# The low-rank pass in blocks of 480 columns, and the first unit's loads, splits and products in one program part with the first norm

## The reference, cut to what matters

```
xn = rmsnorm(x, norm_mix_pre)
p  = xn @ w_in          # RWKV r,k,v (3 x 2048), low-rank w,a,g (96+96+256), DeltaNet q,k,v, z, beta, alpha (16+16), two gates
y_A = RWKV-7 time mixing; decay, a and gate come from the low-rank columns: tanh(lw) @ w2, la @ a2, sigmoid(lg) @ g2
y_B = gated DeltaNet; beta = sigmoid(p_beta), g = -exp(a_log) * softplus(p_alpha + dt_bias)
x  = x + rmsnorm((sigmoid(gA) * y_A + sigmoid(gB) * y_B) @ w_out)
x  = x + rmsnorm(swiglu(rmsnorm(x)))
```

## Time and profile before

| | |
|---|---|
| median of 3 runs | 2353.65 us |
| the profiled execution, its own time | 2358.39 us |
| its span, first to last instruction | 2356.5 us |
| mean granted TensorE clock | 0.948 |
| TensorE matmuls busy | 2161.3 us (92%) |
| VectorE, ScalarE, GpSimd busy | 1414.1, 1086.9, 158.2 us |

### The profile page before, as it was taken

How to read it: one execution, slowest core, us unless ns; L and a number is a source line. 1 busy time by engine, 2 the same in 40 slices (tenths; PEclk the granted TensorE clock), 3 DMA queues, 4 the chain that set the end, 5 groups by cost and what they waited for, 6 DMA issues and landing times. The chain is left out here.

```text
span 2356.5 us, 51465 instructions
## 1 busy us (share of the span) xinstructions
PE 2161.3 (92%) x19523; PEld 1862.1 (79%) x19523; DVE 1414.1 (60%) x2772; ACT 1086.9 (46%) x2019; POOL 158.2 (7%) x277
## 2 busy tenths in 40 slices
PE   5699999999999999999999966939999999999995
PEld 5698888888888888888888854838888888878884
DVE  3276687778677766867776754444554544444444
ACT  4354555545554545555454533344444444434443
POOL 2000110110011011101101110000000000000000
PEclk8699999999999999999999966969999999999998
DMA  4654545444444545444544304426655555545452
GB/s 114 155 143 116 138 111 132 123 125 125 115 116 123 129 113 139 113 113 123 130 114 113 87 5 185 154 90 197 195 182 192 181 192 182 174 165 191 178 184 101
DMA packets 388239, 327.32 MB, mean 139 GB/s; under 512 B 15360, under 2 KB 328160, under 8 KB 381408
## 3 DMA queue, kind: packets, MB, share of 16 engines
q1 hardware_dynamic: 376304, 319.16, 46.5%
q10 hardware_dynamic: 11760, 5.41, 0.9%
HBM read 322.44 MB, written 2.10 MB: 138 GB/s over the span
## 5 line engine op out<-in xcount | busy, mean ns | idle before, releaser
L1489 DVE TENSOR_TENSOR wlo<-wr,whi 128x1024 fp32r<-128x1024 f32 x296 | 362.4, 1225 | 436.0 <-ACT whi L1484 436.0
L232 PE MATMUL ps<-hi,xh 128*128 128x384 f32 (+1 forms) x1600 | 581.7, 364 | 42.8 <-DVE lo L218 24.4
L234 PE MATMUL ps<-hi,xl 128*128 128x384 f32 (+1 forms) x1600 | 548.9, 343 | 0.0
L233 PE MATMUL ps<-lo,xh 128*128 128x384 f32 (+1 forms) x1600 | 548.1, 343 | 0.0
L1484 ACT ACTIVATE whi<-wr 128x1024 fp32r<-128x1024 f32 x296 | 313.5, 1060 | 493.2 <-PE ps L1502 484.9
L218 DVE TENSOR_TENSOR lo<-raw,hi 128x768 fp32r<-128x768 f32 (+1 forms) x400 | 378.1, 964 | 147.6 <-ACT hi L213 144.0
L213 ACT ACTIVATE hi<-raw 128x768 fp32r<-128x768 f32 (+1 forms) x400 | 328.1, 834 | 245.8 <-PE ps L234 235.4
L232 PEld LDWEIGHTS ps<-hi,xh 128*128 128x128 f32 x1600 | 311.1, 194 | 76.4 <-issue 47.7
L1498 PE MATMUL ps<-whi,xh 128*128 128x512 f32 x832 | 328.1, 394 | 20.5 <-DVE wlo L1489 20.5
L1502 PE MATMUL ps<-whi,xl 128*128 128x512 f32 x832 | 326.9, 393 | 0.0
L1500 PE MATMUL ps<-wlo,xh 128*128 128x512 f32 x832 | 326.5, 392 | 0.0
(11 more groups left out here) (284 smaller groups left out, 2396.1 us busy)
## 6 DMA issues: line engine op xcount, KB each, us to landing
raw<-in_w_in SPq DMA_DIRECT2D x294, 512.0 KB, 5.5
wr<-in_ffn_w_gate SPq DMA_DIRECT2D x44, 1024.0 KB, 5.2
wr<-in_ffn_w_up SPq DMA_DIRECT2D x44, 1024.0 KB, 5.2
wr<-in_ffn_w_down SPq DMA_DIRECT2D x22, 2048.0 KB, 7.7
wr<-in_w_out SPq DMA_DIRECT2D x16, 1024.0 KB, 5.2
xt<-in_x SPq DMA_DIRECT2D x1, 2048.0 KB, 8.0
x<-in_x SPq DMA_DIRECT2D x1, 2048.0 KB, 15.8
out_x<-y SPq DMA_DIRECT2D x1, 2048.0 KB, 7.0
```

The lines of the kernel that those rows point to most:

```text
L232: nc.tensor.matmul(o, xh[:, kc, xs], hi[q % QBUF][:, k, 0:w], start=kc == 0, stop=False)
L233: nc.tensor.matmul(o, xh[:, kc, xs], lo[q % QBUF][:, k, 0:w], start=False, stop=False)
L234: last = nc.tensor.matmul(o, xl[:, kc, xs], hi[q % QBUF][:, k, 0:w], start=False, stop=kc == KC - 1)
L1489: nc.vector.tensor_tensor(wlo[s.par][:], src, whi[s.par][:].bitcast(F32), ALU.subtract).then_inc(s.lo, 1)
```

## The change

1. The low-rank pass is cut by contraction blocks: 16 quanta of one block with all 480 columns (`project_lora`, 6 matmuls of 480 columns each), in 4 fills of 4 blocks, each loaded by three transfers (224, 224 and 32 columns).
2. SyncE's list of part 1 begins with x in two halves, each with its own semaphore, then the four low-rank fills, then the six fills of unit 0. The 14 row loads, the 7 small loads and unit 0's 5 small weights are issued by ScalarE, at three places of its list. TensorE's wait for the parameter rows counts these 14 alone (`rows_in`); the rows are turned in PSUM bank 7.
3. The norm: a root chain for each half of x, and x is scaled on VectorE. VectorE first copies the parameters (`par`).
4. TensorE waits before a low-rank quantum for the xl group that it reads, not for the last. The first four hi splits and the first lo split stand ahead of the transposes.
5. Unit 0's 20 splits, 18 quanta and two take-outs move from part 2 to part 1, around the tail; the barrier stands behind them.

```diff
-                    sp.dma_start(xt[:], a["x"][0].rearrange("(t p) n -> p t n", p=P)).then_inc(x_in, 16)
...
+                    for t in range(NT):
+                        sp.dma_start(xt[:, t, :], a["x"][0][t * P:(t + 1) * P, :]).then_inc(x_in[t], 16)
                     for fill in range(4):
...
+                        for at, col, n in ((0, COL_LORA, 224), (224, COL_LORA + 224, 224), (448, COL_BETA, 32)):
...
+                    load_unit_weights(sp, 0)
...
+        def project_lora(pe, q):
+
+            pe.wait_ge(lo_ready, count(None, q + 1))
+            for t in range(NT):
+                last = product(ps[:, 4 + t, 0:LW], q, t, split_of(hi, None, q), split_of(lo, None, q))
             last.then_inc(quantum_done, 1)
...
+                    dve.wait_ge(Pe.sem, Pe.after("par"))
+                    step("par", nc.vector.tensor_copy(par2[:, 0:352], ps[:, 7, 0:352]))
+                    for t in range(NT):
+                        one = slice(t, t + 1)
+                        dve.wait_ge(A.sem, A.after(f"ss{t}"))
+                        step(f"var{t}", nc.vector.tensor_scalar(ss[:, one], ss[:, one], 1.0 / D, NORM_EPS, ALU.mult, ALU.add))
+                        rsqrt(nc, dve, D_, f"rs{t}_", 0, rx[:, one], ss[:, one], rt[:, one])
+                        D_.step(f"xs{t}", nc.vector.tensor_scalar(xt[:, t, :], xt[:, t, :], rx[:, one], None, ALU.mult))
+                    split_lo(dve, None, 0)
                     transpose_x_dve(dve, D_, A, NORM1)
...
-                    pe.wait_ge(D_.sem, D_.after("lo7"))
                     for q in range(QL):
-                        project(pe, None, q, PW if q < 8 else 96)
+                        pe.wait_ge(D_.sem, D_.after(f"lo{q // 2}"))
+                        project_lora(pe, q)
+                    for q in range(4):
+                        project(pe, 0, q)
                     pe.wait_ge(pass_out, 2)
...
+                    for q in range(4, FIRST):
+                        project(pe, 0, q)
```

More of the change, by code:

```diff
@@ L136, in build @@
         small_in = sem("small_in")
+        rows_in = sem("rows_in")
         tiles = sem("tiles")
-        x_in = sem("x_in")
+        x_in = [sem(f"x_in{i}") for i in range(2)]
         masks_made = sem("masks_made")
@@ L268, in transpose_x_pe, with transpose_x_act @@
                 done.step(f"x{g}", last)
-        def transpose_x_act(act, done, turned, weight):
-            for g in G8:
+        def transpose_x_act(act, done, turned, weight, groups=G8):
+            for g in groups:
                 act.wait_ge(turned.sem, turned.after(f"x{g}"))
@@ L354, in _ @@
[L354 to L360, removed]
@@ L449, in _ @@
                                                               accum_out=ss[:, t:t + 1]))
-                    act.wait_ge(D_.sem, D_.after("rs10"))
-                    for t in range(NT):
-                        A.step(f"xs{t}", nc.scalar.activation(xt[:, t, :], xt[:, t, :], ACT.Copy,
-                                                              scale=rx[:, t:t + 1]))
-                    act.wait_ge(D_.sem, D_.after("par"))
-                    transpose_x_act(act, A, Pe, NORM1)
-                    for q in range(QL):
-                        split_hi(act, None, q, PW if q < 8 else 96)
@@ new lines, in _ @@
+                    split_hi(act, None, QBUF)
+                    with nc.allow_non_contiguous_dma(reason="a few hundred single values"):
+                        for i, (c0, n) in enumerate(lora_cols):
+                            act.dma_start(lmix[0:n, i:i + 1],
+                                          mix[3 * D + c0:3 * D + c0 + n].rearrange("(p a) -> p a", a=1)
+                                          ).then_inc(small_in, 16)
+                    act.dma_start(alog[:], a["gdn_a_log"][0].partition_broadcast(P)).then_inc(small_in, 16)
@@ L464, in _ @@
+                    act.wait_ge(quantum_done, QL)
+                    for t in range(NT):
+                        nc.scalar.activation(lp[:, t, :], ps[:, 4 + t, 0:LW], ACT.Copy).then_inc(pass_out, 1)
+                    for q in range(2, 6):
+                        split_hi(act, 0, q)
                     act.wait_ge(Pe.sem, Pe.after("lora"))
@@ L527, in _ @@
                         ALU.mult, ALU.mult))
+                    for q in range(11, FIRST + LEAD):
+                        split_lo(dve, 0, q)
                 @block.tensor
@@ L1428, in _ @@
                 def _(act):
-                    for q in range(FIRST + LEAD):
-                        split_hi(act, 0, q)
-                        if q % 8 == 1 and q > 8:
-                            take_out(act, 0, q // 8 - 1)
                     mix_act(act, 0, False, True)
@@ L1440, in _ @@
                 def _(dve):
-                    for q in range(FIRST + LEAD):
-                        split_lo(dve, 0, q)
                     mix_dve(dve, 0, False, True)
@@ L1450, in _ @@
                 def _(pe):
-                    for q in range(FIRST):
-                        project(pe, 0, q)
                     mix_pe(pe, 0, False, True)
```

151 lines of the change are left out of this document (86 added, 65 removed).

## The result

The changed kernel takes 2369.34 us (median of 9 runs, 2357.32 to 2387.25), against 2353.65 us before (9 runs, 2351.14 to 2361.63). The ratio is 1.007, with a 95% interval of 1.0037 to 1.0102: slower by 0.7%. The forecast was 2316.7 us in a range of 2309 to 2328. The profiled execution took 2384.83 us, at a mean granted clock of 0.945.

A forecast was written before the change was run, and what follows sets the result against it. TensorE, 92% busy, was taken as the bound. A shorter low-rank pass and unit 0 overlapped with the tail, less a later norm, were to start the mix 37.0 us earlier: 2353.65 - 37.0 = 2316.7 us, range 2309 to 2328.

The forecast's parts named there:

- The norm: Start of the prologue: parameter rows copied at 12.5 us, turning x starts at 20.3, 0.8 us later than before, a cost.
- The upper bound of 2.3 us for the scaling: Scaling x on VectorE: at most 2.3 us, from the two-operand split's 958 ns for 768 elements; 1.25 us was taken.
- The low-rank pass: TensorE's 16 quanta of 480 columns: quantum 1 starts at 29.7 us, the pass ends at 51.5, against 67.8 before.
- The 5.6 us at the low clock: Start of the low-rank pass: TensorE at 1.2 GHz for 5.6 us, 2.3 quanta; pass ends at 49 if fast throughout.
- Unit 0 and the tail: From 51.5 us, unit 0's 18 quanta with the tail's steps between splits: 42.3 us with waits, to 93.8.
- Sum of the prologue: Everything before the mix: its first TensorE instruction moves from 131.9 to 94.9 us, a gain of 37.0 us.
- late rows: Rival, chance 0.08: ScalarE's row loads come through only with SyncE's traffic; parameters copied at 21 us, all 8.5 later: 2325.
- the tail: Rival, chance 0.15: more of the tail is seen, 2325 us, or the clock stays low longer, 2330.
- an overlap that fails: Rival, chance 0.05: unit 0's overlap with the tail fails, only the shorter low-rank pass gains, 15 us: 2339.
- the marks: Signs expected in the changed timeline: parameter copy about 12 us, x turned near 20, `pu` near 94, then 81 us units.
- The rival "slower": Chance 0.02: the mix, starting 37 us earlier, has low-clock falls 6 us longer in each of 15 units: about 2361.

## Why the prediction was wrong

The norm: turning x was to start at 20.3 and starts at 21.53. The rows land at 12.66, where I took 11.1, and are copied at 14.05, where I took 12.5: 1.55 us late. The scaling takes 1.36 and 1.29 us where I took 1.25; a root chain takes 2.42 us (14.08 to 16.50) where I took 2.53. Right in kind, 1.2 us late in sum. (The upper bound of 2.3 us for the scaling was a slip: 956 ns for 768 elements is 2.55 for 2048. It decided nothing.)

The low-rank pass: quantum 1 stands behind lo at 30.9, where 29.7 was forecast; quanta are 1.30 us apart (32.55, 33.85), where 1.28 was. The 5.6 us at the low clock did not come: the granted clock is 1.00 over the whole pass, the lower bound of that term. The pass ends at 50.5, not 51.5, because the low clock that was taken and did not come is more than the late start.

Unit 0 and the tail: TensorE is idle for 42.80 - 39.65 = 3.15 us of the stretch from 50.5 to 93.3: 0.96 at each of the two ends of a pass, 0.53 and 0.37 at lo 6 and lo 7, where 0.6 and 0.8 were forecast, and 0.33 at the barrier, where 1.1 was. Sum of the prologue: 38.6 us, not 37.0. None of the rivals about it (late rows, the tail, an overlap that fails) came.

**The step that failed is the one that was never worked out: that from the barrier on everything stays as it was.** The sum ends with "the mix is where it was at 131.86", and the marks with "from there the same 81 us per unit". The mix's instructions are the same, and their places in TensorE's code are not. The change takes 179 TensorE instructions away in front of the loop (2634 to 2455). That moved the crossing from the 123rd to the 46th instruction, and TensorE reached it about 2.7 us before it could go on. The price in the profiled run: 34.4 us of stall, and 64.8 - 34.4 = 30.4 us for the clock, for which the 71.8 us more at half speed account (35.9 of work at most). That execution is 15 us above the median. Over the medians the changed kernel is 50.7 us above the same kernel with 50 instructions in front, and 38 of gain less 51 of loss is about the slower result (13 us by these, 15.7 between the medians).

The rival "slower" had a chance of 0.02 and a price of 2361. It named the clock's falls and asked 6 us more of them per unit; the run has 5.5 us more in each of 13 units, on the mean. But it put this down to the earlier start of the mix. Held back by 2.3 us, the kernel stalls as before; with the crossing moved and the start kept, it does not. The last sentence of the marks did hold: "if the time differs while these marks hold, the cause is in the mix".

A sign of it stood in the profile of before: up to 1.6 us of idle time "issue" at the loop's head, and an instruction queue with 161 packets:

```profile
PE ps L769 <- issue: 10.4, 7, 1.6
```

I read the first as a wait for `gb` or as nothing, and the second not at all. The Trainium skill (Runtime: NRT & Kernel Launch, Instruction fetch mechanics) says that code is fetched ahead in blocks of 16 KB, that crossing into a new one is mostly hidden, and that a branch to code outside the window has to wait for a fetch. The traces agree on the size of the packets and on the wait at the jump, 1.7 us in each iteration. The same section says that "Prefetch is purely sequential"; the loops of 2035 and 2051 instructions, whose blocks are fetched again in each iteration, agree, and the loops of up to 421 instructions are fetched no more than once. It doesn't speak of the block behind the jump's target, which is where 34 us went.

What is shown: the stall depends on the count of TensorE instructions in front of the loop, is there in either kernel at the same placement, repeats after 256, and is gone without the jump; each time it ends 2.3 to 2.8 us after the start of an instruction packet. What is argued from these: that the second block is asked for only when the first has come. The two packets of an iteration start 4.4 to 6.4 us apart in the kernels with the loop, 5.6 in the median, and TensorE starts the head 2.6 to 3.4 us after the first; that fits it. Why the clock does not fall in 4 of the 13 stalls, and so why the changed kernel scatters over 30 us when the kernel with 50 in front scatters over 4, stays open. The length of the stall doesn't decide it: stalls of 2.77, 2.82 and 3.09 us pass without a fall, and one of 1.67 has one.

## What to carry to other kernels

In a kernel whose TensorE loop is long and dense, where the loop's code lies can set part of the time: here code added or removed in front of it cost 2 to 4% without touching it (2369.3 and 2403.6 us, against 2318.6). When an edit moves the time and every changed stretch is as planned, look for an idle time "issue" that recurs once per iteration, and test it with a few dummy instructions in front of the loop, or by writing the loop out on that engine. A stall of this kind moves with these instructions; the last section shows waits "issue" that do not. Here the written-out loop is the better cure: it was as fast within 6 us at the two placements tried, and at 2294 us it is 2.5% faster than the kernel before and 3.2% faster than the changed one (2294.0 / 2369.3 = 0.968, from two sets of runs). The kernel before gained 0.5% by the same edit.

## What the runs showed of the hardware

A jump back costs TensorE 1.7 us of idle time in this loop, and the next 256-instruction block is usable about 5.5 us after the loop's first instruction (5.2 to 5.9 in 58 of 78 stalls, 4.2 to 6.2 in all). Both belong to a loop of 2051 instructions, whose code is fetched in each iteration; the loops of up to 421 instructions in the same kernels show no packet.

Not every wait "issue" is one for code. The timeline of the kernel with 50 in front, last unit, where each line is 48 matmuls of 32 rows:

```profile
1355.68 0.84 PE L720 MATMUL ps<-yc,xs 32*32 32x16 f32 x48 [2.38 <-issue]
1356.98 0.83 PE L720 MATMUL ps<-xi,tr 32*32 32x16 f32 x48 [0.46 <-DVE xi L1118]
1361.21 0.83 PE L720 MATMUL ps<-yc,xs 32*32 32x16 f32 x48 [3.39 <-issue]
...
1365.15 0.84 PE L720 MATMUL ps<-yc,xs 32*32 32x16 f32 x48 [1.81 <-issue]
```

All kernels have these waits, about 10 us in sum. They stand at the same instructions of the last unit in all fourteen traces, with 2.1 to 2.4, 3.4 and 1.6 to 1.8 us, though the blocks end at other places from kernel to kernel, and no packet of the instruction queue starts at a fixed time ahead of them. So they are not the stall of this document; what they wait for the profile doesn't name.

TensorE's clock read 1.00 over the whole low-rank pass right behind 1.9 us of idle time. In the kernel before it rose only 5.9 us into dense work behind 5.29 us of idle time, and 5.6 us into it behind the 10.3 us of the load stretch.
